# A decoder layer with gathered experts on one core: an earlier signal for the row numbers, and the next block's front spread over 108 of 128 experts instead of 123

## What is computed

```python
q  = (xt @ wq).reshape(T, PEER_HEADS, 2, D_HALF)
sc = jnp.einsum('thcd,cnd->thcn', q, subkeys)
sv, si = lax.top_k(sc, PEER_TOPK)                       # 16 best of 128, twice
cv, ci = lax.top_k(sum of the 16 x 16 pairs, PEER_TOPK) # 16 best of 256
eidx = the expert's row number;  gate = softmax(cv)
act  = gelu(sum_d U[eidx] * x) * gate
out  = sum_k act[k] * V[eidx[k]]                        # 128 experts a row
```

## Time and profile before

| What | Number |
|---|---|
| median of the runs before | 4305.08 us (4286.76 to 4305.62) |
| the profiled execution | 4314.72 us |
| its span in the trace | 4313.0 us |
| busy: PE, DVE, POOL, ACT | 70%, 71%, 55%, 19% |
| mean DMA rate over the span | 326 GB/s |
| hand-overs between blocks (`px` copies) | 8, the first at 295.0, the last at 3708.3 us |

### The profile page before, as it was taken

The page is one execution under the profiler, slowest core; times in us unless marked ns, Lnnn a source line. Parts: engine busy times, 40 slices in busy tenths (PEclk is TensorE's granted clock), DMA queues, the critical chain, the costliest instruction groups (busy, mean ns, idle before and its releaser), DMA issues.

```text
span 4313.0 us, 36619 instructions
## 1 busy us (share of the span) xinstructions
PE 3039.9 (70%) x11666; PEld 1725.5 (40%) x11666; DVE 3057.9 (71%) x6003; ACT 826.1 (19%) x1738; POOL 2392.4 (55%) x2110
## 2 busy tenths in 40 slices
PE   5746786759666686758766687758866687754776
PEld 3632553326432454326532364325532364211342
DVE  2475969468775978568684978669684888668792
ACT  2111211221121211212111211212111211211111
POOL 1025766556554755567554765557554665566651
PEclk8977888979889788879878888889988798887778
DMA  5249899989999999999999899899999899898985
GB/s 162 74 172 362 331 361 357 366 310 330 382 330 336 325 334 375 339 348 335 353 340 358 315 344 379 325 348 334 371 339 368 304 364 373 329 350 328 367 315 212
DMA packets 457408, 1406.55 MB, mean 326 GB/s; under 512 B 44377, under 2 KB 55929, under 8 KB 457218
## 3 DMA queue, kind: packets, MB, share of 16 engines
q0 software_dynamic: 297216, 1082.26, 67.8%
q1 hardware_dynamic: 147778, 274.54, 17.9%
q10 hardware_dynamic: 12224, 47.41, 3.0%
HBM read 1386.84 MB, written 9.93 MB: 324 GB/s over the span
## 4 chain that ended last, share of the span: by engine, by line
PE 39%; DVE 29%; DMA 17%; issue 8%; ACT 5%; POOL 2%; DVEq 0%; ACTq 0%; POOLq 0%; SPq 0%
PE peer_acc L888 13%; PE bank L681 10%; DMA wbuf<-in_w_in_dram 10%; DVE uring L1588 6%; DVE accv L1581 4%; DMA wbuf<-in_peer_wq_dram 4%; PE bank L812 2%; PE bank L694 2%; DMA wbuf<-in_ple_gate_w_dram 2%; PE bank L649 2%; PE bank L810 2%; PE bank L796 2%; DVE feat L1420 1%; PE bank L814 1%; PE bank L869 1%
## 5 line engine op out<-in xcount | busy, mean ns | idle before, releaser
L614 POOL DMA_INDIRECT vring<-in_peer_v_dram,eidx x1024 | 1193.0, 1165 | 1109.9 <-PE peer_acc L888 857.6
L888 PE MATMUL peer_acc<-vring,dg 128*128 128x512 f32 x2368 | 1277.9, 684 | 457.4 <-ACT dg L930 429.6
L605 POOL DMA_INDIRECT uring<-in_peer_u_dram,eidx x1024 | 1169.8, 1142 | 715.1 <-issue 286.6
L1588 DVE CUSTOM_DVE_ANT_0 uring<-uring,px 128x1024 f32<-128x1024 f32 x1024 | 1243.5, 1222 | 78.2 <-DMA uring<-in_peer_u_dram,eidx 57.4
L888 PEld LDWEIGHTS peer_acc<-vring,dg 128*128 128x128 f32 x2368 | 490.0, 219 | 1062.5 <-issue 563.0
L681 PE MATMUL bank<-wbuf,xT 128*128 128x512 f32 (+3 forms) x1440 | 703.3, 638 | 227.0 <-DMA wbuf<-in_w_in_dram 184.9
L1581 DVE SCALAR_TENSOR_TENSOR accv<-vring,pact,accv 128x1024 f32<-128x1024 f32 x424 | 546.0, 1288 | 3.5 <-issue 1.5
L681 PEld LDWEIGHTS bank<-wbuf,xT 128*128 128x128 f32 (+1 forms) x1440 | 275.5, 200 | 639.4 <-issue 354.8
L1569 DVE TENSOR_TENSOR pact<-pg,pgate 128x4 f32<-128x4 f32 x256 | 40.5, 158 | 479.8 <-ACT pg L930 479.7
L694 PE MATMUL bank<-xT,wbuf 128*128 128x128 f32 (+1 forms) x2304 | 299.7, 289 | 51.4 <-DMA wbuf<-in_peer_wq_dram 39.3
L694 PEld LDWEIGHTS bank<-xT,wbuf 128*128 128x128 f32 x2304 | 293.7, 209 | 75.3 <-DMA wbuf<-in_peer_wq_dram 44.9
(11 more groups left out here) (279 smaller groups left out, 3188.7 us busy)
## 6 DMA issues: line engine op xcount, KB each, us to landing
wbuf<-in_w_in_dram SPq DMA_DIRECT2D x198, 512.0 KB, 12.4
wbuf<-in_peer_wq_dram SPq DMA_DIRECT2D x144, 512.0 KB, 10.5
wbuf<-in_w_out_dram SPq DMA_DIRECT2D x72, 512.0 KB, 6.4
wbuf<-in_ple_gate_w_dram SPq DMA_DIRECT2D x72, 512.0 KB, 8.9
uring<-in_peer_u_dram,eidx POOLq DMA_INDIRECT x1024, 6.6
vring<-in_peer_v_dram,eidx POOLq DMA_INDIRECT x1024, 6.5
wbuf<-in_ple_w_dram SPq DMA_DIRECT2D x18, 512.0 KB, 9.1
feat<-in_shift_mu_dram ACTq DMA_DIRECT2D x9, 896.0 KB, 10.0
```

The costliest lines, as they stand in the source:

```text
L605: gp.indirect_dma_start(uring[:, s, :], None, peer_u, row_of(i, n, j)).then_inc(sig(f"u{s}_full"), 16)
L614: gp.indirect_dma_start(vring[:, s, :], None, peer_v, row_of(i, n, j)).then_inc(sig(f"v{s}_full"), 16)
L888: last = mm(acc[c][:, :], dg[:, n % 2, at, :], vring[:, s, c * 512:(c + 1) * 512], start=(n + at == 0), stop=(n == UNITS - 1 and j == pe_e ...
L1588: v.tensor_tensor_reduce(out=uring[:, s, :], in0=uring[:, s, :], in1=px[:, :], scale=1.0, scalar=0.0, op0=ALU.mult, op1=ALU.add, accum_out ...
```

## The change

`SPREAD` goes from 123 to 108, so every stage of tail and front is due after fewer experts, and the last one after expert 107; 20 experts without a stage follow. `PE_SHARE` is re-cut: the four-of-four share runs over units 22 to 27 instead of 26 to 31, and units 28 to 31 go half to TensorE and half to DVE. The experts on TensorE are 74 a block in both. A new semaphore `rows_ready` is incremented by DVE as soon as `eidx` is written, ahead of the wait for the exponentials and the three instructions that normalise `gate`; POOL waits for it at a block's start instead of for `topk_done`. The other users of `topk_done` are as before.

```diff
-SPREAD = 123
+SPREAD = 108
-PE_SHARE = {0: 2, 3: 1, 9: 3, 13: 2, 26: 4}
+PE_SHARE = {0: 2, 3: 1, 9: 3, 13: 2, 22: 4, 28: 2}
...
                 if n == 0 and j == 0:
-                    gp.wait_ge(sig("topk_done"), i)
+                    gp.wait_ge(sig("rows_ready"), i)
                     for jj in range(UNIT):
                         gather_u(i, 0, jj)
...
                 link(v.tensor_copy(eidx[0:n, at:at + HK], e1[0:n, :]))
+                ve.sem_inc(sig("rows_ready"), 1)
                 ve.wait_ge(sig("cv_exp"), i + 1)
```

## The result

The changed kernel takes 4506.1 us (4492.0 to 4534.3) against 4296.8 us (4286.8 to 4305.6) for the kernel before in the same comparison: 1.0496 times as long, 95% interval 1.0435 to 1.0557. It is slower, as forecast, but by 209 us instead of 70, and outside the range that ended at 4455.

A forecast was written before the change was run, and what follows sets the result against it. DVE was taken to bound S2 and S4, the projections' chain S1. Per iteration 38.4 - 18.2 - 11.3 = +8.9 us; eight times, less 0.9, is +70, so 4305 + 70 = 4375 us; range 4250 to 4455.

The forecast's parts named there:

- The early signal: POOL's wait for row numbers at a block's start: worth 0.9 us once, at the first block, and nothing elsewhere.
- S1: Stretch of the projections' chain: 11.3 us shorter, 9.3 from a shorter hand-over and 2 from the second gate product.
- the weights stop being late: Rival: TensorE's 22.0 us of waiting for `w_in` in S1 vanishes, 4200 us, or 4244 with three quarters; chance 0.24.
- S1 goes by bytes: Rival: DMA bytes set S1, so four experts fewer save another 11.7 us; 4282 us, no change; chance 0.14.
- S4: Stretch with DVE 96% busy: loses 4 dot products and 3 sums, 8.8 us of work, so 8.4 us shorter.
- S3: Stretch of the recurrent core's end and `w_out`, DVE 58% busy: loses one dot product, 0.7 us shorter.
- S5: Block's end, experts without a stage, five becoming twenty: 29 gathers at 1.32 us, from 7.7 to 46.1 us, +38.4.
- TensorE pacing S5: Rival: 16 TensorE sums in S5 at a slow clock outlast the gathers; 4537 us, halfway 4450; chance 0.10.
- S2: Stretch with DVE 92% busy: loses 6 dot products and 2 sums, 9.9 us of work, so 9.1 us shorter.
- Nothing in these stretches gets longer by the new shares: S2 to S4: the new shares lengthen nothing, since TensorE's 74 experts a block are the same.
- at 92%: S2: DVE's busy share used as price, so 9.9 us of DVE work taken out returns 9.1 us.
- The bound of a third lost to the chains: S2 to S4, worst case: chains between TensorE and DVE keep a third, so 12 us come back instead of 18.2.

The follow-up runs named there:

- the earlier units: The changed kernel with the units where TensorE takes three of four experts moved from 9-12 to 8-10; 1.0426 times the kernel before.

## Why the prediction was right in direction and wrong in size

**The early signal: right.** Forecast 0.9 us once, measured 1.0004 with an interval of 0.4%. POOL's timeline showed it arriving at the wait seven microseconds late, and nothing in the runs made it earlier.

**S1: right in size, and in the main for the reason given.** -12.0 us against -11.3. The hand-over, the larger part of it, is in DVE's timeline after:

```profile
2330.51 0.69 DVE L1514 COPY px<-z 128x1024 f32<-128x1024 f32 x1
2331.23 1.23 DVE L1589 CUSTOM_DVE_ANT_0 uring<-uring,px 128x1024 f32<-128x1024 f32 x1
...
2333.63 1.29 DVE L1535 TENSOR_TENSOR x<-peer_acc,x 128x512 f32<-128x512 f32 x2
```

4.4 us from the copy's start to the end of `t_sum` at 2334.92, forecast 4.6; neither the first u nor `peer_acc` is waited for. That is 9.5 us less than the 13.9 before. The shares alone shorten S1 by 8.9 us and the spread alone by 6.4; the two overlap, since the spread alone already ends the wait for `peer_acc`. Of the 2 us counted for the second gate product the trace shows 0.9: it waits for its weights now, and from the end of `t_sum` to its end are 34.8 us against 35.7. Where the rest of the 12.0 lies stays open. The two rivals that S1 would have carried fall together. The waits of TensorE in S1 after answer to the earlier trace rows:

```profile
PE bank L681 <- DMA wbuf<-in_w_in_dram: 24.1, 10, 6.1
```

24.1 us against 22.0: the weights are as late as before, though fewer experts' gathers stand beside them. Neither "the weights stop being late" nor "S1 goes by bytes" happened.

**S4: right.** -9.1 against -8.4. **S3** gave 4.6 instead of 0.7; what the other four microseconds are stays open, but the kernel with the signal alone, which is no faster, has 2.2 of them (77.1 against 79.3), so part of it is how executions differ.

**S5: right in mechanism, 6.7 us too small.** The forecast was 29 gathers at 1.32 us plus 7.8 us to the hand-over. Measured are 32 at 1.44 plus 7.96 (2322.55 to 2330.51). Three gathers more are some 4 us: the forecast put the rings one place short of full, 12 u and 16 v and one, but 14 u and 18 v were still to come, so u was six experts ahead and v two. The pace was read where DVE mostly stands still, and in S5 it works beside POOL; that is the rest. The upper bound, +45.5, was just high enough for the measured +45.1.

**TensorE pacing S5: did not happen.** POOL waits 0.6 us for `peer_acc` in S5, at a granted clock of 0.81. The clock was lower than in S4 (0.88), but not near the feared 0.53 to 0.66. TensorE's 39.26 us busy for 69 records, four a sum, are 2.3 us a sum, just under the 2.4 from which it would have decided, so the sums still ran beside the gathers.

**S2: wrong, the step that sank the size.** -9.1 us forecast, +5.1 measured. Two steps failed, both in the rounds of the recurrent core. "Nothing in these stretches gets longer by the new shares" held the number of TensorE's experts to be enough. The spread moved the stages under a table and an order that count experts, so that an evacuation stands behind diagonals that are not ready (2.9 us), the records behind that wait run at a lower clock (1.7 us), and one expert's sums more stand between the rounds (1.8 us): 60.9 us instead of 54.5. And the price "at 92%" was a mean over two parts of S2 with different limits. Ahead of the rounds it nearly held: the change has 3.2 us of DVE's work less there (77.38 to 74.18) and is 2.0 shorter, and with the earlier units 5.8 us less (77.38 to 71.62) gave 5.6. In the rounds it did not: there TensorE's own program is as long as DVE's work was, and 3.4 us of DVE's work less (53.56 to 50.21) gave nothing. The bound of a third lost to the chains was meant for this and was too mild, since it did not let the stretch grow.

By the forecast's own rule 15.7 us an iteration more, eight times, is 126 us: 4375 + 126 = 4501, against 4506 measured. That this comes so near is in part luck. The first iteration grew by 20.8 us and the stretch behind the last hand-over by 9.8, not by 24.6 each, and the profiled executions differ by 32 us less than the medians.

## What to carry to other kernels

A table that is keyed to one loop's counter moves against everything that is keyed to another: when the spacing of the stages changes, ask for each entry what now stands beside it, not only how many there are. A busy share of 92% says that the engine is nearly always at work, not that each microsecond taken off it comes back; cut the stretch where the kind of work changes, and ask in each piece how long the chain is that the engine hides. An engine that waits for nothing but the answers to its own work is that chain: here TensorE, through all of the rounds. And work that hides in the waits of other stages is nearly free there, while at the end of a block the same work costs its slowest resource in full, here two gathers or 2.7 us an expert instead of 1.2 to 1.9.

## What the hardware showed that was not expected

An indirect gather of 128 rows costs POOL 0.94 us and a gap of 0.30 us whether a row has 2 KB or 4 KB: the stretch stayed at 54 us while the rate fell from 360 to 189 GB/s. A gather that begins while one of DVE's two-input instructions runs ends some 0.81 us behind that instruction's end (535 of 549 within 0.02 us) and in S5 takes up to 1.98 us, while the instruction itself is no longer. With DVE's dot products shortened the same stretch reached 393 GB/s at a DMA share of 1.01, above the 360 that had looked like the limit of its DMA. And 3.58 us of waiting cost TensorE 1.7 us more behind it, at a granted clock of 0.68 over the next 5.4 us against 1.00 in the rest of the rounds.
